# A group of 64-place experts served second, lists made nearer to their use, and eight zero products at the start of a hybrid MoE layer

## The reference

```python
    h2 = rmsnorm(x, g_ffn[i]).reshape(T, D)
    idx, wts = route(h2, w_router[i], router_bias[i])        # sigmoid top-8 of 64, group-limited
    moe = routed_experts(h2, idx, wts, w_exp_gate[i], w_exp_up[i], w_exp_down[i]) \
        + swiglu(h2, w_sh_gate[i], w_sh_up[i], w_sh_down[i])
    x = x + moe.reshape(B, S, D)
    ple_gate = jax.nn.sigmoid(rmsnorm(x, g_ple[i]) @ w_ple_gate[i])
    x = x + ple_gate * rmsnorm(p[i] @ w_ple_proj[i], g_ple_post[i])
```

## Time and profile before

| | us |
|---|---|
| median of 3 runs | 985.17 |
| lowest, highest | 983.69, 985.89 |
| the profiled execution, whole | 985.45 |
| its span in the trace | 983.6 |

### The profile page before, as it was taken

One profiled execution on the slowest core, in us unless ns is written; L12 is line 12 of the kernel. 1 busy time (PEld: TensorE's weight loads), 2 busy tenths in 40 slices (PEclk: granted clock), 3 DMA queues, 4 the chain that ended last, 5 costly groups with the idle time before them and its releaser, 6 DMA issues.

```text
span 983.6 us, 15761 instructions
## 1 busy us (share of the span) xinstructions
PE 937.1 (95%) x6411; PEld 492.3 (50%) x6411; DVE 361.7 (37%) x776; ACT 162.7 (17%) x304; POOL 226.5 (23%) x344
## 2 busy tenths in 40 slices
PE   9999999999999999999999999999889899897798
PEld 8688888888556533333333333344323233332344
DVE  3765674336436733333332110111101111111687
ACT  2001234210011211111111111111101112121021
POOL 4216923262000212222222222212111211201110
PEclk9999999999999999999999999999989999999899
DMA  9940006322472799999999999999999999999972
GB/s 335 329 128 1 1 1 208 135 86 79 142 304 107 242 383 395 395 418 400 404 421 411 402 417 409 411 420 422 415 421 422 421 419 416 421 398 372 368 274 86
DMA packets 83913, 301.06 MB, mean 306 GB/s; under 512 B 9299, under 2 KB 35959, under 8 KB 59648
## 3 DMA queue, kind: packets, MB, share of 16 engines
q1 hardware_dynamic: 70144, 263.19, 68.0%
q0 software_dynamic: 11920, 33.63, 8.8%
q10 hardware_dynamic: 1776, 3.21, 0.9%
HBM read 279.26 MB, written 29.36 MB: 314 GB/s over the span
## 4 chain that ended last, share of the span: by engine, by line
PE 74%; DMA 21%; SPq 2%; DVE 2%; issue 1%; ACT 0%; ACTq 0%
PE ps L2273 22%; DMA ring<-in_w_exp_up 18%; PE ps L1876 12%; PE ps L2302 8%; PE ps L2026 6%; PE ps L2005 5%; PE ps L2417 4%; PE ps L1785 2%; PE ps L1818 2%; DMA ring<-in_w_exp_down 2%; PE ps L2097 1%; PE ps L1828 1%; DMA ring<-accumulator 1%; SPq L548 1%; PE ps L2282 1%; SPq L534 1%
## 5 line engine op out<-in xcount | busy, mean ns | idle before, releaser
L2273 PE MATMUL ps<-ring,gates 128*32 128x512 f32 x2560 | 287.0, 600 | 27.3 <-DMA ring<-in_w_exp_up 26.5
L2273 PEld LDWEIGHTS ps<-ring,gates 128*32 128x32 f32 x2560 | 88.2, 111 | 218.0 <-issue 217.1
L2302 PE MATMUL ps<-ring,poolbuf 128*32 128x512 f32 x1280 | 147.3, 601 | 3.0 <-DMA ring<-in_w_exp_down 2.1
L1599 DVE COPY poolbuf<-ps 128x256 f32<-128x256 f32 x40 | 17.0, 425 | 355.9 <-PE ps L2282 355.9
L800 POOL TENSOR_TENSOR tickets<-cst 128x1 f32<-128x1 f32 x77 | 14.6, 189 | 397.4 <-ACT actT L1003 392.0
L2302 PEld LDWEIGHTS ps<-ring,poolbuf 128*32 128x32 f32 x1280 | 38.3, 110 | 84.6 <-issue 83.0
L1003 ACT ACTIVATE actT<-ps,qT 128x1024 f32<-128x1024 f32 x40 | 44.6, 1114 | 143.9 <-PE ps L2302 143.9
L995 ACT ACTIVATE poolbuf<-ps 128x256 f32<-128x256 f32 x40 | 15.4, 384 | 278.8 <-PE ps L2273 278.8
L1876 PE MATMUL ps<-xrow,ring 128*128 128x256 f32 x256 | 57.9, 381 | 0.1
L2026 PE MATMUL ps<-ring,gates 128*128 128x512 f32 x128 | 56.4, 594 | 0.0
L1876 PEld LDWEIGHTS ps<-xrow,ring 128*128 128x128 f32 x256 | 48.3, 190 | 8.5 <-issue 1.7
(11 more groups left out here) (303 smaller groups left out, 1072.3 us busy)
## 6 DMA issues: line engine op xcount, KB each, us to landing
ring<-in_w_exp_down SPq DMA_DIRECT2D x64, 1024.0 KB, 17.4
ring<-in_w_exp_gate SPq DMA_DIRECT2D x62, 1024.0 KB, 13.3
ring<-in_w_exp_up SPq DMA_DIRECT2D x62, 1024.0 KB, 16.3
ring<-accumulator SPq DMA_DIRECT2D x12, 1024.0 KB, 13.2
ring<-in_w_gate SPq DMA_DIRECT2D x8, 1024.0 KB, 11.7
ring<-in_w_in SPq DMA_DIRECT2D x5, 1024.0 KB, 10.1
xrow<-in_x SPq DMA_DIRECT2D x8, 512.0 KB, 6.4
accumulator<-ring SPq DMA_DIRECT2D x1, 4096.0 KB, 19.5
```

Of the source, the lines that this page charges most:

```text
L2273: last = mm(bank(2 + k)[part, :], hgT[k][:, q, part], pair_view(EXPERT_SLOT[js[c]])[:, q], start=(q == 0), stop=(q == KD - 1))
L2302: last = mm(bank(6 + half)[part, :], eactT[r % 2][:, q, part], w[:, q, half * 512:(half + 1) * 512], start=(q == 0), stop=(q == 1))
```

## The change

Group 1 (`EARLY`) now has 64 places for each expert and serves the experts of ranks 32 to 35; groups 2 to 8 have 96 and serve ranks 4 to 31, groups 9 to 15 have 64 as before. There are still 40 steps: 0 to 2, 3 and 4, then three for each of groups 2 to 8 (5 to 25), then two each. The order comes from a new row of constants, `RANK_AT`, with which `perm` is made. The order of the loads (`load_group`) follows the groups' sizes. The list of group g is made in step `LIST_STEP[g]` (1, 2, 4, 7, 10, 13, 15, then 16 to 23) and no longer in step g. The raising of the ranks is done in two parts, the early group's ahead of its places. `WARMING` goes from 14 to 8. The steps of the jobs keep their numbers.

```diff
-WARMING = 14
+WARMING = 8
...
+EARLY = 1
 CAP2 = 64
 LESS = CAP - CAP2
-STEP_OF = [(g, s) for g in range(NGROUP) for s in range(GROUP * (CAP if g < BIG_GROUPS else CAP2) // P)]
+LARGE = [g for g in range(BIG_GROUPS + 1) if g != EARLY]
+STEP_OF = [(g, s) for g in range(NGROUP) for s in range(GROUP * (CAP if g in LARGE else CAP2) // P)]
...
+LIST_STEP = [0, 1, 2, 4, 7, 10, 13, 15] + [2 * BIG_GROUPS + n for n in range(NGROUP - BIG_GROUPS)]
+LIST_OF = {LIST_STEP[g]: g for g in range(1, NGROUP)}
...
+RANK_AT = list(range(GROUP)) + list(range(GROUP * BIG_GROUPS, GROUP * BIG_GROUPS + GROUP)) + \
+    list(range(GROUP, GROUP * BIG_GROUPS)) + list(range(GROUP * BIG_GROUPS + GROUP, NE))
...
+    c[:, C_RANK:C_RANK + NE] = RANK_AT
...
-                    if g - 1 >= BIG_GROUPS:
+                    if g - 1 not in LARGE:
                         load_in(pos + 1, e[1])
...
-                if e and g - 1 < BIG_GROUPS:
+                if e and g - 1 in LARGE:
...
-            nc.vector.tensor_scalar(perm, cst[0:NE, C_IOTA:C_IOTA + NE], pos_col, None, ALU.is_equal
+            nc.vector.tensor_scalar(perm, cst[0:NE, C_RANK:C_RANK + NE], pos_col, None, ALU.is_equal
...
-            link(nc.vector.tensor_reduce(small[0:1, 34:35], cnt_row[:, 0:SMALL], AX_X, ALU.max))
-            link(nc.vector.tensor_reduce(small[0:1, 35:36], cnt_row[:, SMALL:NE], AX_X, ALU.max))
+            link(nc.vector.tensor_reduce(small[0:1, 34:35], cnt_row, AX_X, ALU.max))
+            link(nc.vector.tensor_reduce(small[0:1, 35:36], cnt_row[:, SMALL[0][0]:SMALL[0][1]], AX_X, ALU.max))
+            link(nc.vector.tensor_reduce(small[0:1, 36:37], cnt_row[:, SMALL[1][0]:SMALL[1][1]], AX_X, ALU.max))
+            link(nc.vector.tensor_tensor(small[0:1, 35:36], small[0:1, 35:36], small[0:1, 36:37], ALU.max))
...
+            def shift_ranks(part, less):
+                own = rank3[:, :, part[0]:part[1]]
+                less3 = less.rearrange("p (i e) -> p i e", i=NT)
+                link(nc.vector.tensor_scalar(less3, own, 0.5, float(LESS), ALU.is_gt, ALU.mult))
+                link(nc.vector.tensor_tensor(own, own, less3, ALU.add))
+
+            shift_ranks(SMALL[0], small[:, 0:NT * GROUP])
             places(1, rank3[:, :, GROUP:2 * GROUP])
             dve.wait_ge(act_moved, 16 + 16 * NT)
-            less3 = rest[:, 0:NT * (NE - SMALL)].rearrange("p (i e) -> p i e", i=NT)
-            link(nc.vector.tensor_scalar(less3, rank3[:, :, SMALL:], 0.5, float(LESS), ALU.is_gt, ALU.mult))
-            link(nc.vector.tensor_tensor(rank3[:, :, SMALL:], rank3[:, :, SMALL:], less3, ALU.add))
+            shift_ranks(SMALL[1], rest[:, 0:NT * (SMALL[1][1] - SMALL[1][0])])
...
-                if 1 <= r < NGROUP:
-                    lists(r)
+                if r in LIST_OF:
+                    lists(LIST_OF[r])
```

More of the change, by code:

```diff
@@ L73 @@
 C_IC = C_PAIR2 + 4
-C_ALL = C_IC + NG * PAD
+C_RANK = C_IC + NG * PAD
+C_ALL = C_RANK + NE
 def jobs_of(step, slot):
@@ L82, in cap_of @@
 def cap_of(g):
-    return CAP if g < BIG_GROUPS else CAP2
+    return CAP if g in LARGE else CAP2
 def steps_of(g):
@@ L118, in constant_table @@
     c[0:NE, C_KEYP] = key
-    for g, at in ((0, C_PAIR), (BIG_GROUPS, C_PAIR2)):
+    for g, at in ((0, C_PAIR), (EARLY, C_PAIR2)):
         for step in range(steps_of(g)):
@@ L1490, in _ @@
             link(nc.vector.tensor_reduce(pos_col, above, AX_X, ALU.add))
-            nc.vector.tensor_scalar(perm, cst[0:NE, C_IOTA:C_IOTA + NE], pos_col, None, ALU.is_equal
+            nc.vector.tensor_scalar(perm, cst[0:NE, C_RANK:C_RANK + NE], pos_col, None, ALU.is_equal
                                     ).then_inc(perm_ready, 1)
-            HEAD, SMALL = NE // 2, BIG_GROUPS * GROUP
+            HEAD, SMALL = NE // 2, ((EARLY * GROUP, EARLY * GROUP + GROUP), (BIG_GROUPS * GROUP + GROUP, NE))
             dve.wait_ge(sorted_ps, 1)
@@ L1554, in weights_of @@
                 w = found[:, :, TCOL:].rearrange("p s (e c) -> p s e c", e=2)
-                own = cst[:, C_PAIR:C_PAIR + 6] if g < BIG_GROUPS else cst[:, C_PAIR2:C_PAIR2 + 4]
+                own = cst[:, C_PAIR:C_PAIR + 6] if g in LARGE else cst[:, C_PAIR2:C_PAIR2 + 4]
                 total = pair_sum[:, 0:n, :, :]
@@ L1634, in _ @@
                     rows_T(r + 1, (r + 1) % 2)
-                if 1 <= r < NGROUP:
-                    dve.wait_ge(list_ps, r + 1)
-                    rows_of(r, found_of(r))
-                    if r == 1:
+                if r in LIST_OF:
+                    g = LIST_OF[r]
+                    dve.wait_ge(list_ps, g + 1)
+                    rows_of(g, found_of(g))
+                    if g == 1:
                         weights_of(0, found_of(0))
-                    weights_of(r, found_of(r))
-                    if r + 1 < NGROUP:
-                        places(r + 1, rank3[:, :, (r + 1) * GROUP:(r + 2) * GROUP])
+                    weights_of(g, found_of(g))
+                    if g + 1 < NGROUP:
+                        places(g + 1, rank3[:, :, (g + 1) * GROUP:(g + 2) * GROUP])
                 for n in jobs_of(r, 0) + jobs_of(r, 1):
```

## The result

| | before | after |
|---|---|---|
| median, us | 985.53 | 992.32 |
| lowest, highest, us | 983.69, 988.70 | 991.07, 993.32 |
| span of the profiled execution, us | 983.6 | 989.6 |

Six runs of each stand behind the table. In the later sets, medians, ratios and intervals leave out three executions that were far slower than the others of their kernel: 1011.41 and 1956.49 us of the changed kernel with 14 zero products, and 3419.78 us of the kernel before. The ratio after to before is 1.0058, with a 95% interval of 1.0044 to 1.0072. A second set of runs of the changed kernel, beside other runs of the kernel before, gave 1.0044 (1.0027 to 1.0061). So the change costs 0.4 to 0.6%, and the forecast of 986.1, with 988.3 as its upper end, was wrong.

The account below looks back on a forecast made before the run. From 375 us TensorE and the transfers were both taken as full, with transfers setting the stage's end. Clock +0.9, fuller queue -1.2 and hole +1.2 gave +0.9 us, a median of 986.1; 8-in-10 range 982.3 to 988.3.

Parts of the forecast that it names:

- What bounds the kernel: Experts' stage from 375 us: TensorE and DMA both full; transfers set its end at 894 us.
- The fuller queue: Steps 3 to 16: earlier slot release deepens the load queue, 411 GB/s instead of 408, -1.2 us (bound -4.5).
- rival 2: Large groups: the deeper queue carries 420 GB/s there too, -4.5 us; time 982.8 to 980.5; chance 0.12.
- The hole: Around step 27's release, 698 to 703 us: loads go out too late, engines lack weights, +1.2 us (0 to 3).
- the debt of one step: Steps 24 to 27: work tied to step numbers lies one step deeper in the transfers' order; step 26 at 673.1.
- Rival 3: Step 27: the gap in the loads is as long as its bound, +3 us; time 987.9, up to 989.5; chance 0.22.
- The lists: List making, now up to steps 16 to 23: same sum, no gather late, cost 0.
- VectorE's added operations: Before step 1: four operations, 0.8 us, fit in VectorE's 2.46 us wait ending at 348.4; cost 0.
- Zero products and clock: Kernel start: q begins at 7.8 us, 1.4 earlier, but at 1.2 GHz, costing 2.3; net +0.9 us (-1.4 to +1.3).
- The sum: Whole kernel: +0.9 clock, -1.2 queue, +1.2 late gap in the loads, together +0.9: 986.35, median 986.1.
- The chances: Whole kernel: faster by over 0.2% 0.22, slower 0.24, within 0.2% 0.54.

Follow-up runs that it names:

- the runs that take it away: Changed kernel with 14 zero products, shared expert's late tiles moved from steps 24 to 27 to 26 to 29: 0.9995 with late lists, 0.9992 with early lists.

## Why the prediction was wrong, point by point

**What bounds the kernel.** Right in the main. From 375 us on the transfers and TensorE are both full, and a hole in the transfers reaches the end: 6.7 us in the window, of which the runs that take it away give back 3.3 to 3.5 by the ratios and 2.4 and 4.9 by the spans. The 2 to 3 us that TensorE lost at the start of one execution of the changed kernel didn't reach it.

**The fuller queue.** The prediction took -1.2, by 411 GB/s in place of 408, and named 415 or more as what would refute it. The execution profiled shows 416, -3.1 us, nearer to the end that rival 2 stood for. TensorE's waits moved ahead as said, 6.8 us in sum from 377 to 536 us where about ten were named; kernel after, steps 5 and 8:

```profile
403.07 8.77 PE L2290 MATMUL ps<-ring,gates 128*32 128x512 f32 x64 [2.01 <-DMA ring<-in_w_exp_up]
...
445.18 8.38 PE L2290 MATMUL ps<-ring,gates 128*32 128x512 f32 x64 [2.94 <-DMA ring<-in_w_exp_up]
```

But the queue's depth isn't shown to be the cause. The kernel before with late lists alone, which has no small group in front, moves 415 in the same stretch and 404 in the next:

```profile
377.15:535.90 158.75, 157.69 (x1522) 59.16 (x1518) 32.96 (x99) 27.23 (x39) 37.83 (x81) 1.00 1.01 415
535.90:648.30 112.40, 108.80 (x1082) 42.84 (x1078) 33.37 (x127) 18.85 (x27) 25.83 (x56) 1.00 1.00 404
```

The early group alone (early lists, 14 zero products), in three variants that are the same up to 630 us, shows 411, 415 and 409. So one execution differs from another by up to 6 GB/s, 2.3 us, and their mean is near the 411 of the forecast. The four profiles with the early group and the late lists together show 413 to 417. What lies above 411 seems to go with the lists, which the prediction put at nothing: a step without one takes 11.75 us instead of 12.13 to 12.33 and releases its slots earlier. With so few profiles that is a hint, not shown.

What neither forecast nor rival had is that the gain is handed back before the late work begins. In GB/s for the two stretches, 377 to 536 and 536 to 648 us: before 408, 412; after 416, 403, and 413, 399 when profiled again; with 14 zero products 416, 394; with early lists 411, 408; with late lists in the kernel before 415, 404; at `EARLY` = 4 410, 415. Summed over both, each of these lies within 2 us of the kernel before. The reason I give for it is argued, not shown: both TensorE and the transfers are full, so once the transfers are ahead TensorE's products set the releases, and the queue can't be fuller than they let it be. What the trace shows of it is that TensorE of the changed kernel waits for nothing from the first product of step 17, at 557.82, to 704 us, with steps 17 to 22 at 12.13 to 12.18 us each, where the kernel before took 11.75 without its waits and still waited for weights. The prediction said that the ring lets nobody run ahead, and did not apply it to the gain.

**The hole.** This is the step that failed, and it carries the result. The prediction had the mechanism, the debt of one step and the late tiles, and had even step 26 at 673.1, measured 675.14. The 2.1 us are in its first term: group 8 was to begin at 628.6, when its weights had landed, and began at 630.70 without a wait, when TensorE had got there by its own products. Three things were then mis-sized.

1. It priced one release, that of step 27, where the earlier trace rows give 8.2 us of reserve. At step 26's release the reserve was 10.1 us; in the changed kernel this release came 9.8 us later (682.50 for 672.72), and the last of the four loads ahead of it landed by 680.6, where the loads ahead landed up to 682.8 before (when the single load of 674.76 landed, the trace doesn't say). So the queue was at its end at that release already, and short at two before it, 663.10 and 674.76. The window from 700 to 704 us, the dip that was forecast, is 4 x (1 - 171/417) = 2.4 us, close to the price given to it as a bound, 3. The other 4.3 of the 6.7 us lie ahead of it. (By the prediction's own terms that bound is 5.6 - 1.9 = 3.7 and not 3; it would not have covered them either.)
2. It compared the release with the landing of the transfers ahead and added 2.8 us for the start of a lone transfer. That is too little of a reserve, and the landings were put too early. In the changed kernel the rate falls to 289 GB/s around the release of 663.10, although the load issued at 655.37 landed only 15.0 us later, at 670.4, a reserve of 7 us; and the loads issued at 687.70 landed up to 702.8, not at 697 to 699, since the holes ahead delayed them too. That left 1 us behind 701.80, and yet the rate is 171 from 700 to 704 us: the weights issued at 701.80 landed 5.1 us later.
3. It let the rows of one or two steps fill what is left. From 680 to 684 us the rate with rows and all is 221 GB/s.

```profile
680.00:684.00 4.00, 4.00 (x42) 2.10 (x37) 1.31 (x3) 0.80 (x2) 0.12 (x1) 1.00 0.75 221
```

The term was +1.2 with 0 to 3 as its ends; it measured +6.7. By the runs that take it away, 1.0028 to 0.9995 and 1.0027 to 0.9992, it is 3.3 to 3.5 us of the end time. Rival 3 named this side, with a price of 3 for the term, less than half of it.

**The lists.** "Cost 0" holds for the kernel before (0.9996). No wait of TensorE for gathered rows shows in the profile after. In the changed kernel they lengthen steps 16 to 23 by 0.38 us each, and step 26's release comes 1.6 us later with them than without; the prediction counted the lists' sum, and not when the steps that carry them release their slots. The end time shows none of it that these runs can tell.

**VectorE's added operations.** Cost 0, nothing speaks against it: TensorE's wait for `gates` ahead of step 1 is 0.7 us in sum, as before.

**Zero products and clock.** The transposes came at 4.91 (forecast 4.95). Q was to start at 7.8 and started at 8.83, as the weight unit landed at 8.70, 7.5 us after its issue instead of 6.6. The 16 products took 6.43 us, and step 0 began at 343.09 for 340.76, so the term was +2.3 instead of +0.9; the forecast had them at half rate for 3.2 to 5.3 us, and the granted clock was 0.50, the lower level, for all of this window:

```profile
8.90:14.30 5.40, 5.40 (x13) 4.32 (x14) 0.00 (x0) 1.15 (x2) 0.04 (x1) 0.50 1.09 367
```

But the reason given was wrong. The clock was not late to rise: it was up by the transposes at 4.91 (eight in 1.16 us, as against 1.97 at the lower level), and it had fallen when q began, behind a wait of 2.76 us. And the step from there to the end failed as well. The ratio with 8 zero products in the kernel before is 0.9995, and in the changed kernel the 2.3 us are taken up before step 26. As for the rule drawn from the Trainium skill, "TensorE: Matmul & The Clock Gate", Part 4, that transposes don't count as busy for the clock gate as products do: in the second execution the zero products end at 4.83, the transposes run at half rate up to 6.85, and q runs at full rate from 8.56 on. No run here tells whether the transposes counted.

**The sum** of the two executions profiled. +2.3 at the start (not paid), -3.1, +2.5, +6.7, and -0.4 for 421 instead of 420 GB/s from 704 to 862 us. The three in the middle give +6.1, the last makes it 5.7; the span grew by 6.0. That it closes is partly luck. The same three stretches give 8.5 in the second execution of the changed kernel (413, 399, 349 GB/s) and 8.4 with 14 zero products (416, 394, 352), whose spans grew by 6.1 and 5.8. In these two step 0 was as early as before or earlier, and they handed back more by 648 us; in all three group 8 begins within 0.3 us (630.70, 630.90, 630.67). So part of the 3.1 us is probably the transfers catching up with the late start. The prediction named the last weight, near 894 to 895; the first load of the last group, 861.93 in the kernel before, shows with 5.3 us how much later the last weights are, kernel after:

```profile
867.24 0.33 SPq L556 DMA_DIRECT2D ring<-in_w_exp_gate  x1
```

**The chances.** 0.24 for slower was too little. The prediction found a loss of up to 3 us and a gain of about 1, and let 3 us stand as the most that the loss could be, although it came from one release out of several.

What stays open: how much of the loss belongs to the 8 zero products. By spans it is 0.2 us, by ratios 1.0058 and 1.0044 against 1.0028, 0.3 and 0.16%, and the intervals of the second set of the changed kernel and of the run with 14 overlap. The times fall into two heaps: with 14 zero products five of ten lie at 988.1 to 989.5 and five at 991.1 to 992.8, with 8 two of 15 at 988.0 and 988.3 and the rest at 991.1 to 993.3. All three profiles are of the upper heap, so what makes the lower one, and whether the zero products decide between them, no trace tells. And no run has 8 zero products with the late work moved.

## What to carry to other kernels

Where loads are released by the consumer's steps and the ring holds one group, list for every release the time it comes and the time the transfers ahead of it land; the difference is the reserve, and a reordering that moves the consumer back by a step takes most of a step's time from each of them (here 9.8 us of a step of 12). Here 8 to 10 us of reserve kept the rate up, and with 7 us and less it fell. Work tied to a step's number, not to the group it lies in, moves with respect to the weights when the groups' sizes are reordered: move it along, or its long steps hold up releases that can't wait. And a lead that the transfers win early in such a stage isn't kept by itself: in every variant here it was gone, or all but gone, at the end.

## What the runs showed of the hardware

TensorE's clock rises at a moment that differs from one execution to the next. With 14 zero products, all of them begun at 1.04 us, the 28 matmuls took from 5.17 to 6.34 us in ten profiles, as the clock rose at about 5 us in some and only at about 7 in others, and q's 16 products behind them took 3.69 to 3.72 in all ten. With 8, q's took 6.43 us in one execution of the changed kernel and 3.69 in another, and 6.30 in the kernel before; with 1 they took 5.42. The clock was up at 4.91 us once and down again at 8.83, behind transposes of 1.16 us and a wait of 2.76.

The executions of one kernel spread by more than the prediction took: 35 runs of the kernel before, one set of three, reach from 983.11 to 991.22 us, and the 95% intervals of ratios over 9 to 12 runs are still 0.11 to 0.17% to either side.
